# A hybrid decoder layer step on one core: the samples' query work moved ahead of the last projection tile, the fourth query tile behind the gate branch, the recurrent squares summed on TensorE

## The reference

```python
h = rms_norm(x, norm1_g) * (1 + scale1) + shift1          # scale, shift: silu(c) @ w_ada
z = h @ w_in
x_lru, g_lru, q_lat, kv_lat, k_rope = jnp.split(z, IN_SPLITS, axis=-1)
hs, h_last = rg_lru(causal_dwconv(x_lru), ...)            # h = a*h + u over the sequence
lru_out = hs * jax.nn.gelu(g_lru)
q = (rms_norm(q_lat, g) @ w_uq).reshape(b, s, 8, 96)      # 64 plain + 32 rotary
q_nope, q_rope = rms_norm(q[..., :64]), apply_rope(rms_norm(q[..., 64:]))
kv = (kv_lat @ w_ukv).reshape(b, s, 8, 128); k_nope = rms_norm(kv[..., :64]); v = kv[..., 64:]
attn = attend(q_nope, q_rope, kv_lat, k_rope)             # prompt: causal; samples: paged cache
mixed = concat([rms_norm(lru_out, lru_out_norm_g), rms_norm(attn, mla_out_norm_g)]) @ w_o
```

## Time and profile before

| | |
|---|---|
| median of 3 runs | 948.32 us (946.69 to 949.16) |
| the profiled execution | 949.23 us, span 947.4 us |
| TensorE (PE) busy | 919.8 us, 97% |
| VectorE (DVE) busy | 637.4 us, 67% |
| ScalarE (ACT) busy | 513.1 us, 54% |
| GpSimd (POOL) busy | 184.3 us, 19% |
| chain that ended last | TensorE 88%, VectorE 6%, ScalarE 2%, DMA 2% |

### The profile page before, as it was taken

The page is one execution under the profiler, slowest core; times in us unless marked ns, Lnnn a source line. Parts: engine busy times, 40 slices in busy tenths (PEclk is TensorE's granted clock), DMA queues, the critical chain, the costliest instruction groups (busy, mean ns, idle before and its releaser), DMA issues.

```text
span 947.4 us, 20112 instructions
## 1 busy us (share of the span) xinstructions
PE 919.8 (97%) x7805; PEld 858.7 (91%) x7805; DVE 637.4 (67%) x1241; ACT 513.1 (54%) x1147; POOL 184.3 (19%) x163
## 2 busy tenths in 40 slices
PE   5899999999999999999999989999999999999998
PEld 3588876799999999999899979999999999999997
DVE  2893378488888888888863667777777777722321
ACT  2414845689889889898863354444444443311111
POOL 0032323333333324333330301100000001000000
PEclk9999999999999999999998999999999999999999
DMA  9996732300212203202130423333333331653202
GB/s 338 332 281 222 223 134 102 146 2 23 91 59 77 90 24 112 90 24 90 46 91 23 113 60 90 89 89 90 92 96 98 97 97 50 161 153 80 63 1 91
DMA packets 107897, 100.12 MB, mean 106 GB/s; under 512 B 7125, under 2 KB 96597, under 8 KB 105770
## 3 DMA queue, kind: packets, MB, share of 16 engines
q1 hardware_dynamic: 104030, 77.91, 28.1%
q0 software_dynamic: 3456, 20.97, 6.2%
q10 hardware_dynamic: 340, 0.27, 0.1%
HBM read 96.41 MB, written 2.94 MB: 105 GB/s over the span
## 4 chain that ended last, share of the span: by engine, by line
PE 88%; DVE 6%; ACT 2%; DMA 2%; issue 1%; SPq 0%; POOL 0%; DVEq 0%; ACTq 0%; POOLq 0%
PE ps L890 51%; PE ps L1286 20%; PE ps L885 6%; PE ps L1247 2%; PE ps L1183 2%; PE ps L923 2%; DMA RW<-w_ada 2%; PE ps L1062 1%; PE ps L896 1%; PE ps L1282 1%; DVE RB L1996 1%; PE ps L1209 1%; DVE input_low L1929 1%; DVE up_weights_low L2371 0%; DVE small L1970 0%
## 5 line engine op out<-in xcount | busy, mean ns | idle before, releaser
L890 PE MATMUL ps<-normed_high,up_weights_high 128*128 128x260 f32 x704 | 142.5, 284 | 2.5 <-DVE normed_low L2392 2.4
L890 PE MATMUL ps<-normed_high,up_weights_low 128*128 128x260 f32 x704 | 142.5, 284 | 0.0
L890 PE MATMUL ps<-normed_low,up_weights_high 128*128 128x260 f32 x704 | 142.1, 284 | 0.0
L1791 ACT ACTIVATE up_weights_high<-RW 128x1024 fp32r<-128x1024 f32 x44 | 46.6, 1061 | 128.0 <-PE ps L890 128.0
L836 POOL TENSOR_TENSOR latents_low<-RB,latents_high 128x512 fp32r<-128x512 f32 x64 | 82.7, 1292 | 165.7 <-ACT latents_high L1667 165.6
L1286 PE MATMUL ps<-key_weights_high,latents_high 128*128 128x260 f32 x512 | 113.3, 302 | 0.1
L890 PEld LDWEIGHTS ps<-normed_high,up_weights_high 128*128 128x128 f32 x704 | 108.9, 189 | 3.1 <-issue 2.2
L890 PEld LDWEIGHTS ps<-normed_high,up_weights_low 128*128 128x128 f32 x704 | 109.1, 189 | 0.0
L890 PEld LDWEIGHTS ps<-normed_low,up_weights_high 128*128 128x128 f32 x704 | 108.7, 189 | 0.0
L1286 PE MATMUL ps<-key_weights_high,latents_low 128*128 128x260 f32 x512 | 103.1, 283 | 0.0
L1286 PE MATMUL ps<-key_weights_low,latents_high 128*128 128x260 f32 x512 | 103.1, 283 | 0.0
(11 more groups left out here) (350 smaller groups left out, 2069.5 us busy)
## 6 DMA issues: line engine op xcount, KB each, us to landing
RW<-w_ada SPq DMA_DIRECT2D x24, 1024.0 KB, 7.0
RW<-w_up SPq DMA_DIRECT2D x44, 512.0 KB, 5.1
RW<-w_down SPq DMA_DIRECT2D x8, 1408.0 KB, 7.3
RW<-w_in SPq DMA_DIRECT2D x11, 512.0 KB, 6.4
RB<-w_o SPq DMA_DIRECT2D x8, 512.0 KB, 4.2
RB<-x_prompt SPq DMA_DIRECT2D x2, 1024.0 KB, 12.2
o_y_p<-RB SPq DMA_DIRECT2D x4, 448.0 KB
cst<-consts SPq DMA_DIRECT2D x1, 844.5 KB, 12.0
```

The source lines that it names most:

```text
L890: last = mm(ps[j % 4][rows[0]:rows[1], h, 0:H], lhsT, src[:, h * H:(h + 1) * H], start=start, stop=stop)
L1791: A(wuH[:, KT * g:KT * g + KT, :], wup[:, c, KT * g:KT * g + KT, :], ACT.Copy).then_inc(s_whi, 1)
```

## The change

- QST moves from behind kv1 to before the third query tile, QA behind that tile and ahead of w11, SPREAD behind w11; the fourth query tile moves from ahead of w11 to behind SPREAD. The slots follow (`IN_ORDER`, `PREP_ORDER`).
- ScalarE copies the last gate tile and does the GELU before it squares the fourth query tile; `rstd(J_NLRU)` moves ahead of the stored rows.
- The recurrent squares are summed by four accumulating products on TensorE; GpSimd's three additions go. NLRU moves from behind the fourth block of stored rows to behind kv1, from slot 1 to slot 3.
- Blocks 0 and 1 of the stored rows stand between kv1, kv2 and kv3, with two fillers behind each; the fillers become 4, 2 and 2 instead of 3 and four times 1.
- The low halves of the key weights are made by GpSimd instead of VectorE. On VectorE the samples' copies and the first `split_queries` come earlier, the third query tile comes behind the scans and the fourth behind the gated product, and `lru_normed` stands before the third key tile's sums.
- `QA` and `QRS` move in SBUF to behind `newrow`, with a gap of their size where they were, since they are now written before w11 is done. Unused semaphores go, and two functions move in the text.

The diff, without the semaphores and with moved functions shown once:

```diff
             + ["gr", "wt", "w6", "r4", "nq", "w7", "c3", "nkv", "w8", "kr0", "w9", "r5", "qs", "kr1", "q0", "q1", "w10", "c4",
-               "q2", "q3", "w11", "kv0", "kv1"])
-PREP_ORDER = [("c5", 3), ("qst", 3), ("kv2", 1), ("qa", 3), ("kv3", 2), ("spread", 0), ("l0", 3), ("l1", 0), ("l2", 3), ("l3", 0),
-              ("nlru", 1), ("l4", 3), ("l5", 0), ("l6", 3)]
+               "qst", "q2", "qa", "w11", "spread", "q3", "kv0", "kv1"])
+PREP_ORDER = [("c5", 3), ("nlru", 3), ("l0", 3), ("kv2", 1), ("l1", 3), ("kv3", 2), ("l2", 3), ("l3", 0), ("l4", 3), ("l5", 0), ("l6", 3)]
...
         prep = sb("prep", [P, 736])
-        QA = sb("QA", [P, NS, HEADS])
-        QRS = sb("QRS", [P, NS, HEADS])
         OLR = sb("OLR", [P, NS, KV])
...
         OL = sb("OL", [P, NS, HEADS])
+        sb("between", [P, 2 * NS * HEADS])
         new_all = sb("newrow", [P, 1088])
+        QA = sb("QA", [P, NS, HEADS])
+        QRS = sb("QRS", [P, NS, HEADS])
         new_sq, new_parts, new_rstd, new_mask, new_lat = [new_all[0:NS, a:b] for a, b in ((0, 512), (512, 640), (640, 648), (648, 656), (768, 896))]
...
                 in_low(n)
+            pool.wait_ge(s_kw, 2)
+            for e in range(2):
+                nc.gpsimd.tensor_tensor(kwL[:, e, :, 0:4 * NOPE], wkn[:, :].rearrange("p (g n) -> p g n", g=2),
+                                        kwH[:, e, :, 0:4 * NOPE].bitcast(F32), ALU.subtract).then_inc(s_kw, 1)
             full(pool, J_WIN[7])
...
-            for k in range(1, LT):
-                pool.wait_ge(s_sq, KT + 4 + k + 1)
-                if k > 1:
-                    pool.wait_ge(s_lrn, k - 1)
-                nc.gpsimd.tensor_tensor(lru_sq[:, 0, :], lru_sq[:, 0, :], lru_sq[:, k, :], ALU.add).then_inc(s_lrn, 1)
...
             mod_columns(4)
-            queries(2)
-            queries(3)
-            w_in(11)
-            later_chunk(15)
-            pe.wait_ge(s_kvn, 1)
-            keys_and_values(0)
-            mod_columns(5)
-            keys_and_values(1)
             claim(pe, J_QST)
...
             last.then_inc(psum_full[J_QST % 4], 1)
+            queries(2)
+            claim(pe, J_QA)
+            pe.wait_ge(s_qg, 4)
+            pe.wait_ge(psum_free[J_WT % 4], free_value(J_WT))
+            for h in range(HEADS):
+                last = mm(flat(J_QA)[:, NS * h:NS * h + NS], keyT[0:NOPE, P * h:P * h + P], gq8[:, h, :], start=True, stop=True)
+            last.then_inc(psum_full[J_QA % 4], 1)
+            w_in(11)
+            later_chunk(15)
+            claim(pe, J_SPREAD)
+            mm(flat(J_SPREAD)[:, 0:NS * HEADS], C("spread", P, R), QRS[NOPE:QK, :, :], start=True, stop=True).then_inc(psum_full[J_SPREAD % 4], 1)
+            queries(3)
+            mod_columns(5)
+            pe.wait_ge(s_kvn, 1)
+            keys_and_values(0)
+            keys_and_values(1)
+            pe.wait_ge(psum_free[J_COL[5] % 4], free_value(J_COL[5]))
+            keep_busy(spare, 4)
...
+            claim(pe, J_NLRU)
+            for k in range(LT):
+                pe.wait_ge(s_sq, KT + 4 + k + 1)
+                last = both(J_NLRU, ones, lru_sq[:, k, :], k == 0, k == LT - 1)
+            last.then_inc(psum_full[J_NLRU % 4], 1)
+            pe.wait_ge(s_kr, 2)
+            stored_rows(0)
+            keep_busy(spare, 2)
             keys_and_values(2)
-            claim(pe, J_QA)
-            pe.wait_ge(s_qg, 4)
-            pe.wait_ge(psum_free[J_WT % 4], free_value(J_WT))
-            for h in range(HEADS):
-                last = mm(flat(J_QA)[:, NS * h:NS * h + NS], keyT[0:NOPE, P * h:P * h + P], gq8[:, h, :], start=True, stop=True)
-            last.then_inc(psum_full[J_QA % 4], 1)
+            stored_rows(1)
+            keep_busy(spare, 2)
             keys_and_values(3)
-            claim(pe, J_SPREAD)
-            mm(flat(J_SPREAD)[:, 0:NS * HEADS], C("spread", P, R), QRS[NOPE:QK, :, :], start=True, stop=True).then_inc(psum_full[J_SPREAD % 4], 1)
-            keep_busy(spare, 3)
-            pe.wait_ge(s_kr, 2)
-            for a in range(4):
+            for a in range(2, 5):
                 stored_rows(a)
-                keep_busy(spare, 1)
-            claim(pe, J_NLRU)
-            pe.wait_ge(s_lrn, LT - 1)
-            both(J_NLRU, ones, lru_sq[:, 0, :], True, True).then_inc(psum_full[J_NLRU % 4], 1)
-            stored_rows(4)
             pe.wait_ge(s_lrud, 1)
...
             prep_rstd(3, 2 * HEADS)
-            prep_squares(J_Q[3], query_sq, HEADS * QK)
-            prep_rstd(4, 2 * HEADS)
             def key_squares(a):
...
+            prep_squares(J_Q[3], query_sq, HEADS * QK)
+            act.wait_ge(s_lrud, 2)
+            lru_squares(0)
+            prep_rstd(4, 2 * HEADS)
+            lru_squares(2)
             key_squares(0)
             key_squares(1)
-            act.wait_ge(s_lrud, 2)
-            lru_squares(0)
             prep_rstd(5, HEADS)
-            lru_squares(2)
             prep_rstd(6, HEADS)
+            rstd(J_NLRU, LW).then_inc(s_rs, 1)
+            stored_rows(0)
             key_squares(2)
+            prep_rstd(7, HEADS)
+            stored_rows(1)
             key_squares(3)
-            prep_rstd(7, HEADS)
-            stored_rows(0)
             prep_rstd(8, HEADS)
-            for a in range(1, 4):
+            for a in range(2, 5):
                 stored_rows(a)
-            rstd(J_NLRU, LW).then_inc(s_rs, 1)
-            stored_rows(4)
             stored_columns(0, 9)
...
+            def lru_normed():
+                for k in range(LT):
+                    V.scalar_tensor_tensor(hT[:, k, :], GG[:, k, :], pr("lru_out_norm_g", k), rs[:, :], MUL, MUL).then_inc(s_mix, 1)
+            def split_queries(u):
+                e = u % 2
+                q = QA[:, u, :].rearrange("p (g h) -> p g h", g=2)
+                V.tensor_copy(kwH[:, e, :, 4 * NOPE:KWW], q).then_inc(s_kwq, 1)
+                dve.wait_ge(s_kwq, 2 * u + 1)
+                V.tensor_tensor(kwL[:, e, :, 4 * NOPE:KWW], q, kwH[:, e, :, 4 * NOPE:KWW].bitcast(F32), SUB).then_inc(s_kwq, 1)
             prep_sums(0, qs_sq, 2)
...
                 prep_query_tile(a)
+            mod_columns(4)
+            full(dve, J_QST)
+            for i in range(2):
+                src = flat(J_QST)[0:QK, P * i:P * i + P].rearrange("p (g n) -> p g n", g=4)[:, :, 0:NS]
+                V.tensor_scalar(gq8[:, i:HEADS:2, :], src[0:NOPE], qscale[0:NOPE, :], None, MUL).then_inc(s_qg, 1)
+                V.tensor_copy(QRS[NOPE:QK, :, i:HEADS:2], src[NOPE:QK].rearrange("p g n -> p n g")).then_inc(s_qg, 1)
+            dve.wait_ge(s_qg, 4)
+            dve.sem_inc(psum_free[J_QST % 4], 1)
             scan(2)
...
                 V.tensor_copy(kwH[:, e, :, 0:4 * NOPE], wk2).then_inc(s_kw, 1)
-            dve.wait_ge(s_kw, 2)
-            for e in range(2):
-                V.tensor_tensor(kwL[:, e, :, 0:4 * NOPE], wk2, kwH[:, e, :, 0:4 * NOPE].bitcast(F32), SUB).then_inc(s_kw, 1)
-            mod_columns(4)
-            for a in range(2, 4):
-                prep_sums(1 + a, query_sq, HEADS)
-                prep_query_tile(a)
-            dve.wait_ge(s_kr, 2)
-            dve.wait_ge(s_qtok, 4)
-            V.tensor_copy(headk[NOPE:QK, :], krT[NOPE:QK, 0:NP]).then_inc(s_krk, 1)
...
-            mod_rows(5)
-            mod_columns(5)
-            dve.wait_ge(s_g, 1)
-            V.tensor_tensor(GG[:, :, :], TA[:, :, :], GG[:, :, :], MUL).then_inc(s_lrud, 1)
...
-            key_sums(0)
-            key_sums(1)
-            prep_keys(0)
-            prep_keys(1)
+            prep_sums(3, query_sq, HEADS)
+            prep_query_tile(2)
             full(dve, J_QA)
             V.tensor_copy(QA[:, :, :].rearrange("p b h -> p h b"), flat(J_QA)[:, 0:NS * HEADS].rearrange("p (h b) -> p h b", h=HEADS)).then_inc(psum_free[J_QA % 4], 1)
-            key_sums(2)
+            dve.wait_ge(psum_free[J_QA % 4], free_value(J_QA))
+            split_queries(0)
+            mod_rows(5)
             full(dve, J_SPREAD)
...
             dve.sem_inc(s_qbd, 1)
-            key_sums(3)
-            prep_keys(2)
-            prep_keys(3)
...
+            dve.wait_ge(s_g, 1)
+            V.tensor_tensor(GG[:, :, :], TA[:, :, :], GG[:, :, :], MUL).then_inc(s_lrud, 1)
+            mod_columns(5)
+            prep_sums(4, query_sq, HEADS)
+            prep_query_tile(3)
+            dve.wait_ge(s_kr, 2)
+            dve.wait_ge(s_qtok, 4)
+            V.tensor_copy(headk[NOPE:QK, :], krT[NOPE:QK, 0:NP]).then_inc(s_krk, 1)
...
+            key_sums(0)
+            key_sums(1)
+            prep_keys(0)
+            prep_keys(1)
+            dve.wait_ge(s_rs, 5)
+            lru_normed()
+            for a in range(2, 4):
+                key_sums(a)
+                prep_keys(a)
...
-            split_queries(0)
             for e in range(2):
...
             st.seq(V.memset(new_scores[:, :, :], NEG))
-            dve.wait_ge(s_rs, 5)
-            lru_normed()
             for u in range(NS):
```

54 lines of the change are left out of this document (12 added, 42 removed).

## The result

The changed kernel took **950.85 us** (median of 9 runs, 949.67 to 952.65), the kernel before 948.32: a ratio of 1.0029, 95% interval 1.0017 to 1.0042. In a second session (experiment 3) the same two stood at 952.30 and 947.23 us, 1.0048 (1.0031 to 1.0066). The change makes the kernel slower by 2.5 to 5 us; the first of these values lies on the edge of what I had called no difference, the second beyond it.

What follows compares the result with a forecast made beforehand. TensorE, 97% busy, was taken as the bound: +2.67 of extra squares, -1.93 of waits and -1.94 of clock gave -1.2; 2.5 us of new waits made it +1.2, so 949.5 us, range 946.7 to 951.5.

Steps and rivals of the forecast that it cites:

- rival 2: Clock falls in the tail, around the first cache transposes: total +3.1 to +3.8 us, slower by 0.33 to 0.40%; chance 0.10.
- Third query tile, QA, w11: Start of the new TensorE order: QA does not wait, and w11 ends at 155.45, 0.4 us earlier than before.
- New wait one: TensorE, after the four recurrent squares, waits 1.0 us for ScalarE to free PSUM slot 3 at 169.5.
- new wait two: TensorE, before the fifth stored row block, waits 1.3 us for ScalarE's read of slot 3, behind kv3's rstd.
- Rival 1: No new waits: TensorE finds slot 3 free, -1.2 us, so 947.1; chance 0.18.
- Covers: Work moved on GpSimd and VectorE costs nothing: low key-weight halves, 1.5 us ahead of the GELU's end, earlier normed rows.
- T0: Start of the first cache transposes, 178.45 before: forecast 179.65, +1.2 us, each microsecond there being one at the end.
- Taken away ... the clock's 1.94: Fourth key tile, kv3: its run at 1.2 GHz instead of 2.4 was taken as gone, -1.94 us.
- Rival 3: QA's 1.95 us alone bring the clock's fall, now inside w11: +3.1 us; chance 0.06.
- No difference behind T0: From the first attention unit on, 765 us untouched: no difference of more than a microsecond arises there.

Runs made afterwards that it cites:

- experiment 3: Both kernels measured once more, unchanged: the changed kernel 952.30 us, the kernel before 947.23, ratio 1.0048.
- Slot 1: Changed kernel with the recurrent squares' sums in PSUM slot 1 instead of 3: 950.21 us, ratio 1.0015 to the kernel before.
- before again: The kernel before, unchanged, run and profiled a second time: 947.75 us, ratio 1.0006 to the kernel before of its session.
- after again: The changed kernel, unchanged, run and profiled a second time: 952.30 us, ratio 1.0048 to the kernel before.
- reads first: Changed kernel with ScalarE's earlier reads of stored rows 2 and 3, ahead of kv3's rstd: 948.09 us, ratio 0.9998 to the kernel before.
- no waits: Changed kernel, recurrent sums in slot 1, no group of four fillers, ScalarE's stored-row reads earlier, VectorE's normed rows last: 949.44 us, ratio 1.0010 to the kernel before.

## Why the prediction was right, and where not

The first median is 1.35 us over the forecast of 949.5 and inside its range; the second session's 952.30 is 0.8 beyond it. Against the kernel before of the same session it is +2.5 and +5.1 us where +1.2 was forecast. That the first lies in the range is in part luck: the range reached so far up only for rival 2's lower price, and in the first pair of profiles falls of the clock far behind the change took back 3.4 of the 4.2 us by which U was later. By its steps:

- **Third query tile, QA, w11.** QA stood directly behind the half query tile, without a wait; the chunk behind w11 began at 10.72 instead of 11.00: 0.3 earlier, 0.4 forecast.
- **New wait one** 1.02 (forecast 1.0), **new wait two** 1.14 (1.3). The chains are as written: ScalarE's logarithm at 169.84, its first read of row block 2 at 179.12 behind the rstd of kv3:

```profile
169.84 0.68 ACT L1470 ACTIVATE rs<-ps,small 128x520 f32<-128x520 f32 x1
...
179.01 0.21 ACT L1575 ACTIVATE FS<-FS 128x8 f32<-128x8 f32 x1
179.12 0.48 ACT L1606 ACTIVATE otok<-ps 128x160 f32<-128x160 f32 x2
```

Slot 1 took the first away and the earlier reads shortened the second to 0.34, so both causes are shown. Rival 1 falls.
- **Covers.** The key weights' low halves began on GpSimd at 150.94 and took 2.54 us, and VectorE stood idle for 1.63 us ahead of the gated product (1.5 forecast). The normed recurrent rows, earlier now, cost nothing.
- **T0.** +1.61 against the profiled execution of before, +1.2 forecast: 0.1 too little in each of four steps (squares, second key tile, fifth block, column blocks). Besides, the sum starts at 144.94, the chain's view of a start that the timeline puts at 144.78, and ends against the timeline's 178.45; in one view throughout the forecast would have been +1.0 and the miss 0.6.
- **The failed step** is "Taken away ... the clock's 1.94". I read one execution and wrote its fall into all of them. It measured 1.66 us (3.58 - 1.92; kv1, which follows no wait, was the wrong row to compare), and one of three profiles of that order (two unchanged, one with more fillers at T0) is without it. Where it doesn't occur, the change has nothing to win there, and T0 is 3.3 us later (35.28 - 32.01). With a fall of 1.66 in every execution of before the sum would have been +1.5 (1.2 + 1.94 - 1.66), and with none +3.1 (1.2 + 1.94); with a chance of the fall the forecast would have lain between the two.
- **Rival 2 came true.** I gave it 0.10. The clock fell at T0, in both profiles of the changed kernel, and made U - T0 5.29 and 4.90 us instead of 3.73: 1.2 to 1.6 us, under the 1.94 to 2.59 I had priced. What I had against it, that 1.00 us of idleness before 177.97 had brought no fall, was again one execution, with a filler behind each row block ahead of it. By the Trainium skill ("TensorE: Matmul & The Clock Gate", section "What's actually happening") slow is the default and activity releases it, and the monitor runs on its own rather than from the kernel's start. The traces are in line with both (same order, same waits, and the fourth key tile at 3.58 or 1.92 us), though no run here singles out the cause.
- **Rival 3** (QA brings the fall into w11) falls: the clock is 1.00 from 145 to 165 us.
- **"No difference behind T0"** failed. The first profile of before had a clock of 0.53 from 497 to 504 us and 0.79 from 552 to 560:

```profile
497.00:504.00 7.00, 7.00 (x41) 0.53 0.26 75
552.00:560.00 8.00, 6.62 (x39) 0.79 0.06 14
```

and that of after 1.00 in both. So the unit that starts 4.2 us later (186.39 and 182.19) ends up 0.8 us later in the spans. That is not the change: before again reads 1.00 in the first stretch, after again 0.75, and the two variants "reads first" and "no waits" 0.61 and 0.55.

The difference therefore adds up from U: 40.3 to 40.6 after, 35.7 or 37.4 before, depending on its own fall: 2.9 to 4.8 us, and 2.5 and 5.1 were measured, with intervals (1.6 to 4.0 and 2.9 to 6.3 us) that overlap it. Each run also lists its mean granted clock. Of 102 runs of the kernel before in the four sessions of the experiments, the 20 at 0.998 or more took 944.88 to 947.64 us (median 946.1), the 50 under 0.992 a median of 949.4. The changed kernel's two at 0.998 took 950.82 and 950.89: 4.7 us more, near the 4.6 between the U of "after, again" and "before, again"; two runs can only bear this out, not show it.

What stays open: how often each fall comes, since three and two profiles are too few to count, and whether the wait of 1.14 us or the small products around it bring the one at T0. Nor was the changed kernel measured in one session with its variants, so what each repair is worth in time is known to 2.5 us only.

## What to carry to other kernels

A stall that one profile shows may belong to that execution: before crediting a change with its removal, take a second profile or compare the runs' granted clocks, and give the stall a chance rather than a presence. A short wait between small products is a place to try one or two wasted products: here three of them cost 0.24 us at T0, and the median came out 1 to 2 us lower, if not clear of the noise, while the reordering that removed the waits lost 2.5 to 5. A wait in front of a shared point may cover a second chain: removing it gains only up to where that chain ends.
